# First stage of a block kernel: modulation weights by column halves, x normed before it is turned

## The reference, cut to what matters

```python
def gmlp_layer(x, c, ada_w, ada_b, norm_g, w_in, ...):
    shift, scale, gate = split(silu(c) @ ada_w + ada_b, 3)      # each 1024 long
    h = rms_norm(x, norm_g) * (1 + scale) + shift
    u, v, z = split(h @ w_in, 3)                                # each 2048 wide
    v = rms_norm(gelu(v), sgu_g)
    ...
    return x + gate * (y @ w_out)
```

## Time and profile before

| | us |
|---|---|
| median of 3 runs | 1885.05 (1885.0 to 1886.49) |
| the profiled execution | 1885.27 |
| its span in the trace | 1883.6 |
| first product of v starts | 39.40 |
| second block of v starts | 64.11 |

### The profile page before, as it was taken

How to read it: one execution, slowest core, us unless ns; L and a number is a source line. 1 busy time by engine, 2 the same in 40 slices (tenths; PEclk the granted TensorE clock), 3 DMA queues, 4 the chain that set the end, 5 groups by cost and what they waited for, 6 DMA issues and landing times.

```text
span 1883.6 us, 22283 instructions
## 1 busy us (share of the span) xinstructions
PE 1822.2 (97%) x8650; PEld 1490.6 (79%) x8650; DVE 975.2 (52%) x1478; ACT 734.3 (39%) x1006; POOL 75.3 (4%) x149
## 2 busy tenths in 40 slices
PE   4999999989999999999999999999999999999998
PEld 3788888866778887878888887987667888888886
DVE  6336666546346566654444325699676453333223
ACT  4446555224255656432332214323553342232222
POOL 1000000000010000000000000000100000000000
PEclk8999999999999999999999999999999999999999
DMA  8446566432587776333333323235753233432321
GB/s 331 142 134 179 179 179 179 139 107 69 141 226 196 204 199 196 90 99 96 96 112 89 112 91 89 90 112 156 201 157 112 89 90 90 110 101 80 121 90 67
DMA packets 253592, 251.44 MB, mean 133 GB/s; under 512 B 7154, under 2 KB 226628, under 8 KB 246340
## 3 DMA queue, kind: packets, MB, share of 16 engines
q1 hardware_dynamic: 238048, 166.25, 30.0%
q0 software_dynamic: 14976, 83.89, 15.3%
q10 hardware_dynamic: 484, 0.16, 0.0%
HBM read 197.83 MB, written 2.11 MB: 106 GB/s over the span
## 4 chain that ended last, share of the span: by engine, by line
PE 91%; DVE 5%; DMA 1%; issue 1%; ACT 1%; POOL 0%; DVEq 0%; ACTq 0%; POOLq 0%
PE acc L745 13%; PE acc L746 13%; PE acc L747 13%; PE sc L1134 6%; PE acc L1134 3%; PE acc L959 3%; PE acc L961 3%; PE acc L960 3%; PE tr L1134 2%; PE ob L1134 2%; PE misc L1134 2%; DMA s_ada_w<-in_a_ada_w 1%; PE sc L745 1%; PE sc L747 1%; PE sc L746 1%
## 5 line engine op out<-in xcount | busy, mean ns | idle before, releaser
L1922 DVE TENSOR_TENSOR s_w_low<-s_raw,s_w_high 128x2048 fp32r<-128x2048 f32 (+1 forms) x127 | 286.8, 2258 | 304.9 <-ACT s_w_high L1396 304.8
L745 PE MATMUL acc<-s_h_high,s_w_high 128*128 128x512 f32 x880 | 345.1, 392 | 1.6 <-DVE s_sg L2517 1.6
L747 PE MATMUL acc<-s_h_high,s_w_low 128*128 128x512 f32 x880 | 342.5, 389 | 0.0
L746 PE MATMUL acc<-s_h_low,s_w_high 128*128 128x512 f32 x880 | 342.5, 389 | 0.0
L1396 ACT ACTIVATE s_w_high<-s_raw 128x2048 fp32r<-128x2048 f32 (+1 forms) x127 | 238.8, 1881 | 204.0 <-PE acc L1134 167.7
L745 PEld LDWEIGHTS acc<-s_h_high,s_w_high 128*128 128x128 f32 x880 | 165.3, 188 | 37.5 <-issue 4.1
L747 PEld LDWEIGHTS acc<-s_h_high,s_w_low 128*128 128x128 f32 x880 | 165.2, 188 | 34.6
L746 PEld LDWEIGHTS acc<-s_h_low,s_w_high 128*128 128x128 f32 x880 | 165.3, 188 | 33.4 <-issue 0.2
L1787 ACT ACTIVATE s_hid_high<-s_hd 128x512 fp32r<-128x512 f32 x44 | 27.8, 632 | 218.9 <-DVE s_hd L2526 118.6
L959 PE MATMUL acc<-s_h_high,s_w_high 128*128 128x512 f32 x256 | 106.5, 416 | 1.4 <-DVE s_v L2211 0.8
L961 PE MATMUL acc<-s_h_high,s_w_low 128*128 128x512 f32 x256 | 100.6, 393 | 0.0
(11 more groups left out here) (477 smaller groups left out, 3396.3 us busy)
## 6 DMA issues: line engine op xcount, KB each, us to landing
s_raw<-in_a_w_in SPq DMA_DIRECT2D x48, 512.0 KB, 4.9
s_w_high<-s_raw POOLq DMA_DIRECT2D x24, 1024.0 KB, 6.5
s_w_low<-s_raw POOLq DMA_DIRECT2D x24, 1024.0 KB, 7.1
s_raw<-in_ffn_w_gate SPq DMA_DIRECT2D x44, 512.0 KB, 4.0
s_raw<-in_ffn_w_up SPq DMA_DIRECT2D x44, 512.0 KB, 5.2
s_raw<-in_ffn_w_down SPq DMA_DIRECT2D x40, 512.0 KB, 4.3
s_raw<-in_w_in SPq DMA_DIRECT2D x36, 512.0 KB, 4.3
s_raw<-in_b_w_in SPq DMA_DIRECT2D x32, 512.0 KB, 5.4
```

Source lines behind the costliest of these rows:

```text
L745: pe.matmul(bank[b][:, :], w_high[:, o:o + P], hi, start=(k == 0), stop=False, skip_group_check=grouped)
L746: pe.matmul(bank[b][:, :], w_high[:, o:o + P], lo, start=False, stop=False, skip_group_check=grouped)
L747: mm = pe.matmul(bank[b][:, :], w_low[:, o:o + P], hi, start=False, stop=(k == nk - 1), skip_group_check=grouped)
L1922: dve.tensor_tensor(w_low[:, w], raw[:, w], w_high[:, w].bitcast(F32), ALU.subtract).then_inc(w_ready, 1)
```

## The change

- **Modulation weights.** They are fetched as 16 tiles of 128x1024 (0.5 MB) instead of eight of 1 MB. The first eight tiles hold columns 0 to 511 of shift and of scale, the other eight columns 512 to 1023. `half_columns(0)` makes the shift and scale columns of slices k = 0 to 3 from the first half, `half_columns(1)` those of k = 4 to 7. The ring stays at five buffers, now of half the size. POOL begins with them after the first weight chunk has landed.
- **Order of transfers.** SP fetches the first weight chunk ahead of x, and issues the small vectors in ACT's place, behind x. The second weight chunk waits for modulation tile 6 of 16, the spatial weights for tile 14.
- **The norm.** There is no diagonal and no spread factor. ACT multiplies x by each token's reciprocal root (`xn`, four instructions of 128x1024), PE turns `xn` per k (`turn_normed`), and ACT makes slice k of h from that bank in two instructions: scale and shift (line 1495 of the new kernel), then the cast. DVE's share of a slice is one subtraction.
- **x itself** is still turned to `xT` for the residual: slices 0 to 3 at once, slices 4 to 7 two by two inside block 0 of v, with their copies on ACT.
- **The first weight chunk** is cast and subtracted whole at the start.

The core of the diff:

```diff
+            chunk_half(0, 0, W["a_in"], AW)
             for t in range(TT):
                 sp.dma_start(xin[:, t * D:(t + 1) * D], x[0, t * P:(t + 1) * P, :]).then_inc(x_landed, 16)
...
-            for k in range(KD):
-                if k >= 5:
-                    pool.wait_ge(ada0_used, k - 4)
-                pool.dma_start(ada0_w[k % 5][:, :], aw[:, k, 0:2 * D]).then_inc(ada0_landed[k % 5], 16)
-
+            pool.wait_ge(w_landed[0], 32)
+            for i in range(2 * KD):
+                h, k = divmod(i, KD)
+                if i >= 5:
+                    pool.wait_ge(ada0_used, i - 4)
+                pool.dma_start(ada0_w[i % 5][:, :].rearrange("p (b n) -> p b n", b=2),
+                               aw[:, k, 0:2 * D].rearrange("p (b n) -> p b n", b=2)[:, :, h * T:(h + 1) * T])\
+                    .then_inc(ada0_landed[i % 5], 16)
...
             def v_block(b):
 
                 for half in range(2):
-                    if b > 0 or half > 0:
-                        chunk(2 * b + half)
+                    chunk(2 * b + half)
+                    if b == 0 and half == 1:
+                        pe.wait_ge(x_stored, KD)
+                        pe.wait_ge(ada0_used, 2 * KD)
+                        ada_sum(ada0_acc, 1, D)
...
+                        if b == 0 and k + 2 < KD:
+                            turn_normed(k + 2)
+                        if b == 0 and k < 2:
+                            if k > 0:
+                                pe.wait_ge(x_stored, TT + 2)
+                            else:
+                                pe.wait_ge(ada_turned, 1)
+                            for r in range(2):
+                                turn_raw(TT + 2 * k + r)
...
+            def first_h(k):
+
+                act.wait_ge(xn_turned, k + 1)
+                act.wait_ge(ada_cols, 1 + k // 4)
+                if k >= 2:
+                    act.wait_ge(h_ready, k - 1)
+                act.activation(n1[k % 2][:, :], xn_bank[k % 2][:, :], ACT.Identity, bias=ada[:, SHIFT_A + k:SHIFT_A + k + 1],
+                               scale=derived[:, A_A + k:A_A + k + 1]).then_inc(h32_ready, 1)
+                high_of(n1[k % 2][:, :], h_high, k, h32_ready, k + 1, h_high_ready)
+
+            for k in range(TT):
+                raw_x(k)
             for k in range(KD):
-                high_of(n1[k % 2][:, :], h_high, k, h32_ready, k + 1, h_high_ready, shift=ada[:, SHIFT_A + k:SHIFT_A + k + 1])
-                if k == 3:
+                first_h(k)
+                if k == 1:
                     high_part(0, 1, 0)
+                if k in (1, 2):
+                    for r in range(2):
+                        raw_x(TT + 2 * (k - 1) + r)
...
+            half_columns(0)
+            for k in range(4):
+                ada0_tile(KD + k)
+                first_low_of(k)
+                if k == 1:
                     low_part(0, 1)
+            for k in range(4, KD):
+                ada0_tile(KD + k)
+            half_columns(1)
+            for k in range(4, KD):
+                first_low_of(k)
```

More of the change, by code:

```diff
@@ L803, in _ @@
                 .then_inc(rows_turned, 1)
-            pe.wait_ge(ada0_used, KD - 2)
+            pe.wait_ge(ada0_used, 4)
             for k in range(WARM):
                 pe.matmul(ob[:, 384:512], ident[:, :], ones[:, :], start=True, stop=True)
-            pe.wait_ge(diag_ready, 1)
-            pe.matmul(misc[:, :], ones[:, :], diag[:, :], start=True, stop=True).then_inc(spread_ready, 1)
-            for b in (1, 0):
-                pe.wait_ge(ada0_used, KD + 1 - b)
-                ada_sum(ada0_acc, b, b * D, (sc[0], ob)[b])
+            pe.wait_ge(xn_ready, TT)
+            for k in range(2):
+                turn_normed(k)
+            pe.wait_ge(ada0_used, KD)
+            ada_sum(ada0_acc, 1, 0)
+            pe.wait_ge(x_stored, TT)
+            pe.wait_ge(cols_ready, 1)
             def v_block(b):
                 for half in range(2):
-                    if b > 0 or half > 0:
-                        chunk(2 * b + half)
+                    chunk(2 * b + half)
[3 more added lines that the diff above has]
+                        ada_sum(ada0_acc, 1, D)
                     for kk in range(4):
                         k = 4 * half + kk
-                        if b == half == 0 and kk < 3:
-                            pe.wait_ge(first_low, kk + 1)
-                        elif b == half == 0:
-                            chunk(0)
                         if b == 0:
@@ L1444, in _ @@
[L1444 to L1457 removed]
+            act.wait_ge(c_turned, 1)
@@ L1458, in _ @@
+            act.activation(tiny[:, 64:72], sc[0][:, 0:KD], ACT.Silu).then_inc(c_ready, 1)
+            high_part(0, 0, 0)
+            act.wait_ge(x_landed, 16 * TT)
+            for t in range(TT):
+                if t >= 2:
+                    act.wait_ge(x_sq, t - 1)
+                act.activation(x_sq_out[t % 2][:, :], xin[:, t * D:(t + 1) * D], ACT.Square,
+                               accum_out=tiny[:, V_SS + t:V_SS + t + 1]).then_inc(x_sq, 1)
             act.wait_ge(ms_ready, 1)
             act.activation(tiny[:, V_RT:V_RT + 4], tiny[:, V_MS:V_MS + 4], ACT.Sqrt).then_inc(root_ready, 1)
-            act.wait_ge(w_landed[0], 32)
@@ L1461, in _, with raw_x @@
-            for k in range(4):
-                act.activation(w_high[:, k * T:(k + 1) * T], raw[:, k * T:(k + 1) * T], ACT.Copy)\
-                   .then_inc(first_high if k < 3 else w_high_ready, 1)
+            act.wait_ge(x_rcp, 1)
+            for t in range(TT):
+                act.activation(xn[:, t * D:(t + 1) * D], xin[:, t * D:(t + 1) * D], ACT.Copy,
+                               scale=tiny[:, V_R + t:V_R + t + 1]).then_inc(xn_ready, 1)
+            def raw_x(k):
+                act.wait_ge(x_turned, k + 1)
+                act.activation(xT[:, k * T:(k + 1) * T], xT_bank[k][:, :], ACT.Copy).then_inc(x_stored, 1)
@@ L2008, in _, with ada0_tile @@
             dve.wait_ge(c_ready, 1)
[L2010 removed]
+            def ada0_tile(i):
+                h, k = divmod(i, KD)
                 ck = tiny[:, 64 + k:65 + k]
[L2013 to L2014 removed]
+                part = slice(h * D, (h + 1) * D)
+                dve.wait_ge(ada0_landed[i % 5], 16 * (i // 5 + 1))
                 if k == 0:
[L2016 removed]
+                    dve.tensor_scalar(ada0_acc[:, part], ada0_w[i % 5][:, :], ck, None, ALU.mult).then_inc(ada0_used, 1)
```

141 lines of the change are left out of this document (63 added, 78 removed).

## The result

| | before | after |
|---|---|---|
| median, us | 1885.77 (1885.0 to 1886.92, 4 runs) | 1898.07 (1897.02 to 1899.2, 4 runs) |
| the profiled execution, us | 1885.27 | 1899.2 |
| its span, us | 1883.6 | 1897.6 |
| first product of v starts | 39.40 | 29.90 |
| last low half of block 1 ends | 53.29 | 62.73 |

The changed kernel is slower by 0.6%: ratio 1.0063, 95% interval 1.0051 to 1.0075. The forecast was 1886.8 and its range ended at 1890.5. The first product did come 9.5 us earlier, but block 2 came 9.2 us later.

The account below looks back on a forecast made before the run. PE was taken as busy almost throughout, block 1's end set by its products and by last low half + 10.5 us. 1885.27 + 0.5 (later block 2) + 1.1 (clock) = 1886.9, kept as 1886.8; range 1883.5 to 1890.5.

Parts of the forecast that it names:

- My share for x: At the start, x was costed between landing alone and the earlier trace's share of about 43%, landing at 13.6.
- X: Time at which x has landed: 13.6 taken, range 12.5 to 15.0; 12.5 made the result 1.1 us smaller.
- First failed step: Slices 4 to 7: ACT makes each in 1.4, so the last low half ends at 54.1, against 53.29 before.
- Second failed step: Block 1, second weight chunk: ACT's cast until 32.2, DVE 2.3 more, done at 34.5.
- Third failed step: PE's clock: 0 to 2.9 us at the first products, 1.1 taken; 0 between slices 3 and 4.
- the seam: Between slices 3 and 4: PE stands from 44.1 to 49.9 with 0.64 us of work.
- last low half + 10.5: End of block 1: the third weight chunk is ready 10.5 us after DVE's last low half, forecast at 64.6.
- signs I had named: First product 29 to 31, slice 4 49 to 53, last low half 53 to 57, cast 6.3 later, block 2 64 to 67.
- the 1.1 that I had charged in front: First slices of block 1: 1.1 us taken for a possible clock fall costing 0 to 2.9 us.
- Rival 1: Clock stays low over the first two slices and their turns: +5, and 0.5, giving 1891; chance 0.11.
- rival 3: Modulation tiles with 2 KB pieces land late, so block 2 starts 7 later: 1892; chance 0.05.
- Rival 2: Tiles 12 to 15 and second columns ready when slice 3 ends, block 2 at 58.8: 1880; chance 0.08.

Follow-up runs that it names:

- e2: Changed kernel with the turns of normed slices 6 and 7 put ahead of slice 4, into two free banks: 1888.52 us, ratio 1.0012.
- e6: Changed kernel with the second chunk cast behind slice 3, its low part behind the second columns, PE's wait behind the second sum: 1898.02 us.
- e8: Changed kernel with early third-chunk fetch, second chunk worked later, normed slice k + 3 turned ahead of slice k's products, raw turns one by one: 1884.59 us.
- e9: Changed kernel with only the PE order of turns of e8, without its early fetch or later second-chunk work: 1887.67 us, ratio 1.0006.
- e3: Changed kernel with both the early chunk fetch of e1 and the moved turns of e2: 1887.94 us, ratio 1.0008.
- e1: Changed kernel with SP issuing the third and fourth weight chunks ahead of its wait for the padded table: 1891.17 us, ratio 1.0024.
- e10: e8 with the second sum ahead of slice 3's products, two raw turns behind slices 5 and 6, third chunk cast ahead of them: 1881.91 us, ratio 0.9976.
- e5: Changed kernel with 28 unused matmuls on PE between blocks 1 and 2 to hold the clock: 1899.02 us, ratio 1.0066.
- e7: Changed kernel with the second-chunk order of e6 and both edits of e3: 1885.57 us, ratio 0.9996.

## Why the prediction was wrong

The front was right. Step by step, forecast and measured: x landed 13.6 and 11.87; tile 7's end 25.8 and 25.8; first product 29.7 and 29.90. My share for x was too low (about 43%; by the bytes of the earlier trace rows, 2.10 of 5.20 MB, it was 40%, which is further off still). From 8 to 12 us the queues of the changed kernel moved:

```profile
q1 hardware_dynamic: 550, 1.23, 79.9%
q0 software_dynamic: 86, 0.35, 24.1%
```

x's queue got 1.23 of 1.58 MB, 78%. The sum by the Trainium skill's rule of turns (DMA: Bandwidth & Descriptors, SWDGE vs HWDGE vs iDMA), X = 12.5, was nearer than mine, and x was faster still. The nearness is luck: the two thirds were worked out for pieces of 2 KB, but q0's 86 packets here carry 4.1 KB each, as much as a packet of x. By the same rule that is a half, 1.2 MB at 0.2 MB per us from 8 on, X = 14.0 (an estimate); the trace does not agree. It was worth nothing: ACT began the scaled x at 19.79, against 20.1 for the roots in the forecast, and tile 7 ended when forecast.

**First failed step: "ACT makes a slice in 1.4, so the last low half ends at 49.85 + 4.2".** It holds only if the turned slices lie ready. PE had slices 6 and 7 behind the products of slices 4 and 5; the order rows ahead of the prediction show this ("One set of turns stands behind each of slices 2 to 5"), and I charged the turns to PE as 0.44 us each and never asked when their results came. From slice 4's start to the last low half it took 10.2 us instead of 4.2: 6 us. The turn of slice 7 stands at 59.93, and slice 7's low half began 2.1 us behind it:

```profile
59.93 0.60 PE L819 MATMUL misc<-s_ident,s_xn 128*128 128x128 f32 x4
```

Of the 6 us, 1.3 are the half clock of slice 4's products, which the turn of slice 6 stood behind, and 4.7 the order. e2 moved only these two turns and got 3.9 us for that distance.

**Second failed step: "the second chunk (ACT's cast until 32.2 ...)".** It took the chunk for landed by 30.3. It was issued at 23.09 and landed at 34.4. From 26 to 29 us, and then from 29 to 35, the queues moved

```profile
q1 hardware_dynamic: 344, 0.68, 72.1%
q0 software_dynamic: 53, 0.18, 17.1%
```

```profile
q0 software_dynamic: 569, 2.08, 90.0%
q1 hardware_dynamic: 163, 0.30, 13.0%
```

so the weight chunk's queue first had 79% and brought 0.76 of its 1.05 MB by 29 us; for the last 0.30, against 2.08 MB of tiles, it needed until 34.4. With it the last low half of slice 3 ended at 42.27 instead of 40.6, the last tile at 48.4 instead of 46.1 (one of the four also took 2.1 us instead of 1.28, beside POOL's work on the spatial weights), and slice 4 began at 52.56 instead of 49.9: 2.7 us. e6 shows that the landing was not the only thing there: without the wait for it, PE's turns, and the half clock in front of them, hold the same place. Where the turns are out of the way, working in place of waiting is worth something: e8 is 3.1 us faster than e9, of which the early fetch explains at most the 0.80 us that PE of e9 waited in front of block 2.

**Third failed step: the clock.** "0" held at the first products, in this execution: it stayed full over 3.40 us of standing (in seven of the nine variants with this pause it did not). "The third chunk's wait of 2.9 hides all of it: 0" failed at the seam. It counted only PE's way to the end of block 1; but the turn of slice 6 stood behind slice 4's products, and so their 1.3 us came on top of the last low half and of the third chunk behind it (counted in the 6 us). In e2, with the turns ahead of slice 4, they hid as forecast, and in e3, with the fetch early as well, 2.4 us of them came to light. And in front of block 2 I had PE stand 2.9 us; it stood 7.09, the clock fell, and nothing hid the 2.8 us behind that.

**Right:** "last low half + 10.5" for the chunk's readiness (10.6 in the changed kernel, 10.5 in e2, 10.7 in e9), and that it is this rule and not the first product that decides. Of the signs I had named, the first product, slice 4 (52.56) and ACT's cast 6.3 us behind the last low half came. The last low half (62.73, not 53 to 57) and block 2 (after 69) said that I was wrong, and so did the last sign: from block 2's start to the end it was 4.8 us more than before, where I had allowed 1. 2.8 of that are the clock in block 2, 2.0 lie behind it. The time from the turns of the spatial weights to the span's end is 1796 to 1799 us in the twelve profiles, so 3 us of scatter that no run explains.

The sum of the misses: 2.7 (slice 4) + 6.0 (slices 6 and 7) puts block 2 at 73.3 instead of 64.6; the clock adds 2.8 and takes away the 1.1 that I had charged in front. 1886.8 + 8.7 + 2.8 - 1.1 = 1897.2, against 1898.07.

**The rivals.** None was this. Rival 1 (clock low over slices 0 and 1) and rival 3 (tiles late) gave 1891 and 1892, each with the wrong mechanism: the clock was full there and the tiles came in time. Rival 1's price was wrong as well: in e1 the clock was at half over slice 0 (from about 30.2 to 33.6), and slice 2 began only 0.17 us later than in the changed kernel (40.69), as its low half came no sooner anyway. Rival 2 (seam hidden, 1880) did not happen because the order of the lists forbade it, as was said against it. But its number, which I gave 0.08, is nearly what the same data flow gives in e10 (1881.9) once PE's list has been put in another order. What lacked was a rival "slices 4 to 7 come in the cadence of PE's products and not of ACT's", which the order rows would have priced: two slices at 3.2 to 5.7 us (DVE's low halves begin at 53.14, 58.85 and 62.04) instead of 1.4.

## What to carry to other kernels

When a step is moved onto a busy in-order engine "just ahead of its use", ask for each of its results who makes something of it first, and how long that takes; the step must stand that much ahead, and its place in the list counts for more than its length (two turns of 0.44 us cost 6.6 us here, 1.3 of them because the products ahead of them ran at half clock). When a wait is removed and the time does not move (e6), look at what the freed engine waits for now: here it was the same engine, PE, in three places one behind the other, and in e6 at half clock besides. A long pause of PE (7.09 us in front of block 2) was paid twice, once as idle time and once as 2.8 us of clock behind it.

## What the runs showed of the hardware

- **The share of a queue is not a constant.** Against tiles of the same kind on q0, q1 got 78% at 8 to 12 us with x (pieces of 4 KB), and with one weight chunk (pieces of 2 KB) first 79% at 26 to 29 us, then 13% at 29 to 35 us. The pieces are the same in the last two, so their size alone does not set the share; no run shows what does.
- **The same pause gives either clock.** In the changed kernel and its nine variants PE stands 3.40 us (3.41 in e5) in front of its first work on slice 0; the changed kernel, e1, e2, e3, e5, e6 and e7 have the same PE list up to there, the other three a set of turns more. Behind it the clock stays full in three profiles (the changed kernel, e9, e10) and is at half in the other seven, for 3.4 to 6.8 us. The first two rows are the changed kernel's, the third is e8's:

```profile
28.00:30.00 2.00, 0.10 (x1) 0.13 (x2) 1.09 (x3) 1.94 (x4) 0.72 (x1) 1.00 1.03 399
30.00:32.00 2.00, 2.00 (x9) 1.65 (x10) 1.55 (x2) 0.36 (x1) 0.72 (x1) 1.00 1.05 410
```

```profile
30.00:32.00 2.00, 1.92 (x8) 1.65 (x9) 2.00 (x3) 1.97 (x4) 0.56 (x1) 0.59 1.05 412
```

So a pause of this length can't be costed at one value; a range from nothing to 3 us was right for it. In front of block 2 the two kernels with a pause of 7.1 to 7.2 us (the changed one and e6) both had the low clock behind it, and so had e5 after 2.44 us.
